# A fused two-block kernel: scanning one projection group ahead, conditioning products spread out, index scores on stacked operands

## What is computed

```python
mod = silu(c) @ w_ada + b_ada                       # 6 x 1024 values
h = rmsnorm(x) * (1 + scale_m) + shift_m
z, xbc, dt_raw, u_pool, gates = split(h @ w_in)     # 2048, 3072, 32, 1024, 2048 columns
xbc = silu(causal_conv(xbc));  dt = softplus(dt_raw + dt_bias)
y = ssd_chunked_scan(x * dt, dt * a, b, c)          # 4 groups of 8 heads x 4 chunks of 128
y = rmsnorm(y * silu(z), per group) @ w_branch_ssd
x = x + gate_m * (sig(g0) * y + sig(g1) * pool(u_pool)) @ w_out   # then the feed-forward part
```

```python
s = einsum('qhd,sd->qhs', q_idx, k_idx) * 64**-0.5   # 8 index heads of 64, one key
score = einsum('qh,qhs->qs', w_idx * 8**-0.5, relu(s));  _, idx = top_k(score, 128)
```

## Time and profile before

| | |
|---|---|
| median of 3 runs | 2499.92 us (2499.48 to 2509.1) |
| profiled execution | 2502.64 us |
| span of its trace | 2500.6 us |
| TensorE, VectorE, ScalarE, GpSimd busy | 96%, 55%, 43%, 16% |
| mean granted TensorE clock | 0.977 |
| chain that ended last: TensorE, VectorE, ScalarE | 82%, 6%, 5% |

### The profile page before, as it was taken

How to read it: one execution, slowest core, us unless ns; L and a number is a source line. 1 busy time by engine, 2 the same in 40 slices (tenths; PEclk the granted TensorE clock), 3 DMA queues, 4 the chain that set the end, 5 groups by cost and what they waited for, 6 DMA issues and landing times.

```text
span 2500.6 us, 41318 instructions
## 1 busy us (share of the span) xinstructions
PE 2396.1 (96%) x15443; PEld 2139.1 (86%) x15443; DVE 1370.8 (55%) x2095; ACT 1062.9 (43%) x1910; POOL 397.1 (16%) x350
## 2 busy tenths in 40 slices
PE   6999999998999999998989999999999989999998
PEld 5778777887899899887868999999988779999987
DVE  5896777223465245457744666643344445766621
ACT  5646764333343233224444333322455554333322
POOL 0000444700410100100121211100100002211100
PEclk8999999999999999998989999999999999999999
DMA  8564433332233352332202233323422112232332
GB/s 291 167 204 103 108 77 85 92 101 83 85 97 93 97 136 86 99 109 57 52 18 64 84 92 86 90 89 91 136 59 62 44 52 85 84 92 85 89 95 92
DMA packets 409481, 238.38 MB, mean 95 GB/s; under 512 B 11434, under 2 KB 400397, under 8 KB 409381
## 3 DMA queue, kind: packets, MB, share of 16 engines
q1 hardware_dynamic: 400549, 202.25, 29.0%
q0 software_dynamic: 8224, 32.61, 3.8%
q10 hardware_dynamic: 608, 2.16, 0.2%
HBM read 234.54 MB, written 5.00 MB: 96 GB/s over the span
## 4 chain that ended last, share of the span: by engine, by line
PE 82%; DVE 6%; ACT 5%; issue 4%; DMA 3%; POOL 0%; SPq 0%; ACTq 0%; DVEq 0%; POOLq 0%
PE PS L508 60%; PE PS L2056 5%; PE PS L1842 3%; DMA w_raw<-in_w_in_dram 2%; ACT w_hi L429 1%; PE PS L2092 1%; PE PS L1857 1%; PE PS L2187 1%; PE PS L1801 1%; PE PS L2134 1%; DVE w_lo L435 1%; PE PS L1921 1%; PE PS L1957 1%; PE PS L2136 1%; PE PS L2071 1%
## 5 line engine op out<-in xcount | busy, mean ns | idle before, releaser
L435 DVE TENSOR_TENSOR w_lo<-w_raw,w_hi 128x1024 fp32r<-128x1024 f32 (+2 forms) x376 | 469.8, 1250 | 631.0 <-ACT w_hi L429 629.7
L508 PE MATMUL PS<-op_hi,w_hi 128*128 128x264 f32 (+3 forms) x2440 | 601.5, 310 | 16.2 <-DVE w_lo L435 13.4
L508 PE MATMUL PS<-op_lo,w_hi 128*128 128x264 f32 (+3 forms) x2440 | 599.0, 309 | 0.0
L508 PE MATMUL PS<-op_hi,w_lo 128*128 128x264 f32 (+3 forms) x2440 | 596.2, 308 | 0.0
L429 ACT ACTIVATE w_hi<-w_raw 128x1024 fp32r<-128x1024 f32 (+2 forms) x376 | 379.4, 1009 | 313.2 <-PE PS L508 261.6
L508 PEld LDWEIGHTS PS<-op_hi,w_hi 128*128 128x128 f32 x2440 | 397.6, 189 | 47.7 <-DVE w_lo L435 16.2
L508 PEld LDWEIGHTS PS<-op_hi,w_lo 128*128 128x128 f32 x2440 | 397.4, 189 | 22.6
L508 PEld LDWEIGHTS PS<-op_lo,w_hi 128*128 128x128 f32 x2440 | 397.0, 189 | 21.8 <-issue 0.5
L508 PE MATMUL PS<-ff_hi,w_lo 128*128 128x512 f32 (+1 forms) x784 | 240.3, 343 | 0.0
L508 PE MATMUL PS<-ff_hi,w_hi 128*128 128x512 f32 (+1 forms) x784 | 239.9, 342 | 0.0
L508 PE MATMUL PS<-ff_lo,w_hi 128*128 128x512 f32 (+1 forms) x784 | 239.9, 342 | 0.0
(11 more groups left out here) (497 smaller groups left out, 3866.2 us busy)
## 6 DMA issues: line engine op xcount, KB each, us to landing
w_raw<-in_w_up_dram SPq DMA_DIRECT2D x120, 512.0 KB, 3.8
w_raw<-in_w_in_dram SPq DMA_DIRECT2D x64, 512.0 KB, 4.1
w_raw<-in_w_down_dram SPq DMA_DIRECT2D x64, 512.0 KB, 3.8
w_ada<-in_w_ada_dram POOLq DMA_DIRECT2D x12, 2048.0 KB, 9.1
decay<-sums_scratch SPq DMA_DIRECT2D x16, 512.0 KB, 5.2
w_raw<-in_w_branch_ssd_dram SPq DMA_DIRECT2D x16, 512.0 KB, 4.0
w_raw<-in_w_in_a_dram SPq DMA_DIRECT2D x16, 512.0 KB, 3.8
w_raw<-in_w_kv_b_dram SPq DMA_DIRECT2D x16, 512.0 KB, 3.9
```

Of the source, the lines that this page charges most:

```text
L435: dve.tensor_tensor(wlo[slot][:, 0:ks, :], wraw[slot][:, 0:ks, :], whi[slot][:, 0:ks, :].bitcast(F32), ALU.subtract).then_inc(sem("w_split ...
L508: last = pe.matmul(a[0:l.cols, h, 0:cn], w[slot][:, k, 0:l.cols], x[:, kk, c0:c0 + cn], start=(j == 0 and k == 0 and w is whi and x is l.h ...
```

## The change

1. dt's split weight gets buffers of its own (`wd_hi`, `wd_lo`). The weight of xbc group 1 is split into slot 0 while the joint group still runs: ScalarE before its fifth h tile, VectorE before the second half of the modulation columns.
2. `modulation(4)` to `modulation(10)` stand after xbc groups 5, 8, ..., 23, `modulation(11)` after z group 0. VectorE spreads the 64 multiply-adds over 22 groups.
3. z group 0 is multiplied, evacuated and split before the loop; step i handles z group i + 1 (u group i - 15 from step 15 on) and step 23 none. `decays(0)` moves behind the first copies of step 0. u group 0 is evacuated at the end of step 15, after the pad.
4. Index queries are stored in fp32r for each head on all 128 rows, the high part on the head's own 64 rows and the low part on the other 64. The key is stored as `ki_hi` twice and `ki_lo` twice. A score is two accumulating fp32r products of 128 rows. The DMA copy of the key is gone.

The program of the sync queue has no edit.

```diff
@@ -227,6 +227,7 @@
...
+        wd_hi, wd_lo = (at(name, [P, 8, HEADS], F32R, A_MISC + i * 1024) for i, name in enumerate(("w_dt_hi", "w_dt_lo")))
@@ -245,9 +246,9 @@
...
-        iq = at("idx_q", [P, 4, T], F32, F + 16896)
+        idx_q = at("idx_q", [P, QH, T], F32R, F + 85568)
+        ki_hi, ki_lo = (at(name, [P, T], F32R, F + 16896 + i * TILE) for i, name in enumerate(("ki_hi", "ki_lo")))
         kwt = at("ki_wi", [P, T], F32, F + 25344)
-        kid = at("ki_twice", [P, T], F32, F + 27456)
@@ -1093,8 +1094,6 @@
...
             pool.memset(sel_allA[:, 24:32], 1.0).then_inc(sem("B_set"), 1)
-            pool.wait_ge(sem("ki_ready"), 1)
-            pool.dma_start(kid[64:128, :], kwt[0:64, :]).then_inc(sem("kid_in"), 16)
@@ -1164,11 +1163,14 @@
...
             for u in range(2):
                 act.wait_ge(sem(f"w_landed{u}"), 16)
-                cn = P if u else L["dt"].cols
-                act.activation(whi[u][:, :, 0:cn], wraw[u][:, :, 0:cn], ACT.Copy).then_inc(sem("w_hi_ready"), 1)
+                hi, cn = (whi[1], P) if u else (wd_hi, HEADS)
+                act.activation(hi[:], wraw[u][:, :, 0:cn], ACT.Copy).then_inc(sem("w_hi_ready"), 1)
...
             for k in range(KD):
+                if k == 4:
+                    act.wait_ge(sem("w_landed0"), 32)
+                    act.activation(whi[0][:], wraw[0][:], ACT.Copy).then_inc(sem("w_hi_ready"), 1)
                 act.wait_ge(sem("mod_ready"), k // 4 + 1)
@@ -1194,7 +1196,8 @@
...
-            evac_loop(act, L["dt"], dt_in)
+            act.wait_ge(sem("units_done"), 1)
+            dt_in(0, 0, 0)
@@ -1236,7 +1239,10 @@
...
-            decays(0)
+            act.wait_ge(sem("ada_acc"), 12)
+            act.wait_ge(sem("units_done"), L["z"].U0 + 1)
+            act.activation(zT[:, 0, :], acc_view(L["z"], 0), ACT.Copy).then_inc(sem("evacuated"), 1)
+            split_hi(act, L["z"], 0, 0, 0)
             for i in range(24):
                 if i < 16:
                     act.wait_ge(sem("ssd_a"), i + 1)
...
                     act.activation(xsb[:], bank(7), ACT.Copy).then_inc(sem("ssd_x"), 1)
+                    if i == 0:
+                        decays(0)
                     if i < 15:
                         decays(i + 1)
-                if i < 16:
-                    l, g = L["z"], i
-                    dst = zT[:, i, :]
+                if i < 15:
+                    l, g = L["z"], i + 1
+                    dst = zT[:, g, :]
                 else:
-                    l, g = L["u"], i - 16
-                    dst = up[:, i - 16, PAD:UPW]
-                    if i == 16:
-                        act.wait_ge(sem("pool_pad"), 1)
-                act.wait_ge(sem("units_done"), l.U0 + g + 1)
-                act.activation(dst, acc_view(l, g % 2), ACT.Copy).then_inc(sem("evacuated"), 1)
-                split_hi(act, l, g // 2, g % 2, 0)
+                    l, g = L["u"], i - 15
+                    dst = up[:, g, PAD:UPW] if g < KD else None
+                if i < 23 and i != 15:
+                    act.wait_ge(sem("units_done"), l.U0 + g + 1)
+                    act.activation(dst, acc_view(l, g % 2), ACT.Copy).then_inc(sem("evacuated"), 1)
+                if i < 23:
+                    split_hi(act, l, g // 2, g % 2, 0)
                 if 1 <= i <= 16:
                     g, c = STEPS[i - 1]
                     act.wait_ge(sem("ssd_t"), i)
                     act.activation(xbc[:, 4 * g:4 * g + 4, c * P:(c + 1) * P],
                                    bank(3).rearrange("p (t n) -> p t n", t=4), ACT.Copy).then_inc(sem("ssd_yT"), 1)
+                if i == 15:
+                    act.wait_ge(sem("pool_pad"), 1)
+                    act.activation(up[:, 0, PAD:UPW], acc_view(L["u"], 0), ACT.Copy).then_inc(sem("evacuated"), 1)
@@ -1356,8 +1367,10 @@
...
                 if name[0] == "i":
-                    act.activation(halves(iq[:, g, :]), src, ACT.Copy).then_inc(sem("evacuated"), 1)
+                    act.activation(halves(idx_q[0:64, 2 * g, :]), src[0:64], ACT.Copy)
+                    act.activation(halves(idx_q[64:128, 2 * g + 1, :]), src[64:128], ACT.Copy).then_inc(sem("idx_hi"), 1)
                 elif name == "kw":
+                    act.wait_ge(sem("evacuated"), l.G0 + g + 2)
                     act.activation(halves(kwt[0:72, :]), src, ACT.Copy).then_inc(sem("evacuated"), 1)
@@ -1443,6 +1456,9 @@
...
+            act.wait_ge(sem("ki_ready"), 1)
+            act.activation(ki_hi[0:64, :], kwt[0:64, :], ACT.Copy)
+            act.activation(ki_hi[64:128, :], kwt[0:64, :], ACT.Copy).then_inc(sem("idx_hi"), 1)
             for s in range(SLOTS_A):
@@ -1732,9 +1748,10 @@
...
                 for u, l in enumerate((L["dt"], L["xbc"])):
-                    for w, x in ((whi, HH), (whi, HL), (wlo, HH)):
-                        last = pe.matmul(acc_view(l, 0, l.cols), w[u][:, k, 0:l.cols], x[:, k, META:T],
-                                         start=(k == 0 and w is whi and x is HH), stop=(k == KD - 1 and w is wlo))
+                    hi, lo = (whi[1], wlo[1]) if u else (wd_hi, wd_lo)
+                    for w, x in ((hi, HH), (hi, HL), (lo, HH)):
+                        last = pe.matmul(acc_view(l, 0, l.cols), w[:, k, :], x[:, k, META:T],
+                                         start=(k == 0 and w is hi and x is HH), stop=(k == KD - 1 and w is lo))
                     if k == KD - 1:
                         last.then_inc(sem("units_done"), 1)
@@ -1755,9 +1772,11 @@
...
-            products(pe, L["xbc"], None, 8, dt_steps, start=1)
-            for n in range(4, 12):
-                modulation(n)
+                if g >= 5 and (g - 5) % 3 == 0:
+                    modulation(4 + (g - 5) // 3)
+            products(pe, L["xbc"], None, NX, dt_steps, start=1)
+            products_of(pe, L["z"], 0, 0)
+            modulation(11)
             pe.wait_ge(sem("mod_ready"), 3)
             pe.wait_ge(sem("dt_tok"), 4)
             pe.wait_ge(sem("conv_out"), NX + 2)
@@ -1777,10 +1796,10 @@
...
-                if i < 16:
-                    products_of(pe, L["z"], i // 2, i % 2)
-                else:
-                    products_of(pe, L["u"], (i - 16) // 2, i % 2)
+                if i < 15:
+                    products_of(pe, L["z"], (i + 1) // 2, (i + 1) % 2)
+                elif i < 23:
+                    products_of(pe, L["u"], (i - 15) // 2, (i + 1) % 2)
@@ -1892,14 +1911,11 @@
...
-                    rows = slice(64 * e, 64 * e + 64)
-                    q, k = iq[rows, h // 2, q0:q0 + nq], (kid if e else kwt)[rows, :]
-                    if nk <= 512:
-                        last = pe.matmul(PS[:, 4 + 2 * e, 0:nk], q, k[:, 0:nk], start=True, stop=True)
-                    else:
-                        for a in range(2):
-                            last = pe.matmul(PS[:, 4 + 2 * e + a, 0:nk // 2], q, k[:, a * nk // 2:(a + 1) * nk // 2],
-                                             start=True, stop=True)
+                    cn = nk if nk <= 512 else nk // 2
+                    for a in range(nk // cn):
+                        for k in (ki_hi, ki_lo):
+                            last = pe.matmul(PS[:, 4 + 2 * e + a, 0:cn], idx_q[:, h, q0:q0 + nq],
+                                             k[:, a * cn:(a + 1) * cn], start=(k is ki_hi), stop=(k is ki_lo))
                     last.then_inc(sem("idx_ps"), 1)
@@ -2019,7 +2035,7 @@
...
-                    pe.wait_ge(sem("kid_in"), 16)
+                    pe.wait_ge(sem("idx_k"), 1)
                 if s < 4:
                     index_scores(s + 1)
@@ -2285,14 +2301,15 @@
...
             for u in range(2):
                 dve.wait_ge(sem("w_hi_ready"), u + 1)
-                cn = P if u else L["dt"].cols
-                dve.tensor_tensor(wlo[u][:, :, 0:cn], wraw[u][:, :, 0:cn], whi[u][:, :, 0:cn].bitcast(F32),
-                                  ALU.subtract).then_inc(sem("w_split"), 1)
+                hi, lo, cn = (whi[1], wlo[1], P) if u else (wd_hi, wd_lo, HEADS)
+                dve.tensor_tensor(lo[:], wraw[u][:, :, 0:cn], hi[:].bitcast(F32), ALU.subtract).then_inc(sem("w_split"), 1)
             for k in range(2):
                 x_lo(k)
             times_c(dve, link, 3, 0, BY_DVE, BY_DVE)
             for k in range(2, 4):
                 x_lo(k)
+            dve.wait_ge(sem("w_hi_ready"), 3)
+            dve.tensor_tensor(wlo[0][:], wraw[0][:], whi[0][:].bitcast(F32), ALU.subtract).then_inc(sem("w_split"), 1)
             dve.wait_ge(sem("ada_done"), 4)
@@ -2314,7 +2331,6 @@
...
-            post_loop(dve, L["dt"])
@@ -2347,8 +2363,10 @@
...
                 dt_steps(g)
-                n, third = 4 + g // 3, g % 3
-                times_c(dve, link, n, *((0, 2), (2, 5), (5, 8))[third])
+                for n in range(4, 12):
+                    k0, k1 = (min(max(64 * x // 22 - 8 * (n - 4), 0), KD) for x in (g, g + 1))
+                    if k0 < k1:
+                        times_c(dve, link, n, k0, k1)
```

(18 more changed lines are left out.)

## The result

The changed kernel takes 2506.92 us (median of 12 runs), the kernel before 2503.15 (12 runs beside them): ratio 1.0019, 95% interval 1.0010 to 1.0027. That is 3.8 us more, where 4.4 were forecast.

A forecast was written before the change was run, and what follows sets the result against it. TensorE, busy 2396.1 of 2500.6 us, was taken as the bound. The terms -0.6 - 1.6 + 9.9 + 0.8 - 4.1 = +4.4 us gave 2507.0 profiled, 2504.3 on the median (+0.2%), range 2494 to 2514.

The forecast's parts named there:

- Start of the projections: Input projections' start: own dt buffers remove a wait and slow projection, -4.0; joint group later, +0.9; sum -3.1 us.
- Conditioning products: Among xbc projections: six products add 5.1 us, filled waits return 2.6 (bounds 0 and 4.7); xbc end at -0.6.
- Rival 4: xbc stage: VectorE's multiply-adds become the bound, +4.2 us, 2508.5; chance 0.12.
- Last xbc tile to the first product: Before the scan: decay-load chain takes 18.1 us instead of 21.25, -3.1; slow projection +1.5; result -1.6 us.
- Scan step 13: ScalarE waits for u 0's load, holding TensorE before step 14: +8.3, slow clock +1.6, together +9.9 us.
- Gates: Steps 15 to 23 and gates: TensorE waits about 5.7 us before the third gate tile; sum +0.8 us.
- Index scores: Index stage: stacked scores take about 1.0 us a head instead of 1.65; -4.1 us in all, bounds 0 and -7.
- the late key: Index stage: VectorE falls behind in the index projections and the key tile comes late, +1.2 us.
- Rival 3: Index scores: giving up side-by-side heads eats the index gain, 2508.4; chance 0.14.
- Rival 2: After step 13's gap the clock stays low, 5.56 us more per half-clock projection, 2515; chance 0.10.
- shows at the other end, where step 23 has none: Scan's end: the projection done early shortens nothing by itself; TensorE reaches the gates one projection (5.56 us) sooner.
- a difference of 0.5%: Whole kernel: a run must differ by about 0.5% (12.5 us) before a measurement tells it from no change.

The follow-up runs named there:

- experiment 8: Kernel before with only dt's own split-weight buffers and the early split: 2498.97 us, ratio 0.9985.
- run 10: Kernel before with only the conditioning products spread over the input groups, scan and dt buffers as before: 2505.16 us, ratio 1.0011.
- experiment 12: run 6 with the spread undone: products 4 to 10 in a row behind the last xbc tile, 11 behind z 0: 2495.76 us, ratio 0.9976.
- experiment 4: Changed kernel with one load moved: sync queue issues u 0's load ahead of decay load 15: 2496.67 us, ratio 0.9972.
- experiment 1: Kernel before with only the changed kernel's stacked index scores: 2500.23 us, ratio 0.9987.
- experiment 2: Changed kernel with the old index scores, all the rest of the change kept: 2511.64 us, ratio 1.0038.
- run 3: Changed kernel with the scan's order undone (no group projected ahead), the rest kept: 2495.31 us, ratio 0.9969.
- run 6: experiment 4 plus the last norm's reciprocal ahead of step 22's weight split and the first two gate tiles written early: 2488.34 us, ratio 0.9941.
- run 7: run 3 plus run 6's two edits at the gates (reciprocal first, first two gate tiles early): 2495.19 us, ratio 0.9970.
- run 9: run 6 with five of VectorE's eight residual scalings moved behind the index key: 2487.87 us, ratio 0.9945.

## Why the prediction was right, step by step

The time and its sign were right: +4.4 forecast, +3.8 measured (interval 2.5 to 6.8). The step that decides it, the load of u 0 that holds TensorE in step 13, was right in cause and in size. Some of the closeness is luck, as three of the smaller terms show. Against the working:

- **Start of the projections, -3.1 (bounds -4.0 and -1.6).** The dt step behind the next projection stands at 60.73 in the trace after and at 63.69 in the one before: -3.0. Right, with both of its halves: the wait gone, and the joint group 0.7 to 0.8 us later where 0.9 were forecast (experiment 8).
- **Conditioning products, +5.1 - 2.6, xbc end at -0.6.** The end came at 193.03 instead of 194.94, -1.9. The mis-sized term is the waits that the products fill. The products are 4.9 us (0.81 each for 0.85); 2.6 of them were taken to be covered, and a net of 1.1 (-1.9 against the -3.0 of the start) means that 3.8 were in this trace. Over all traces it is nearly all 4.9: from the dt step to the end of the xbc tiles nine with the spread took 131.0 to 132.3 us, and five without it 131.3 to 131.8. The upper bound was 4.7, and I took about half of it. VectorE's idle of 1.62 us once in three groups was the sign that TensorE's products were free there. Rival 4 is out by experiments 10 and 12.
- **Last xbc tile to the first product, 18.1 us.** Measured 18.28 (193.03 to 211.31), with a gap of 2.94 us where 2.7 were forecast; right. The slow clock behind the gap was put at 1.5 and cost twice that: the 16 products took 3.67 instead of 2.00 us, the projection behind them was slow as well, and of a lead of 4.88 us (211.31 for 216.19) 1.75 were left at the transposes of step 0's output (222.66 for 224.41), so 3.1. The term of -1.6 came out at +0.2, outside its bounds. Luck covered it: the term before it was 1.3 us better than forecast, so the two together gave -1.75 where the sum had -2.2.
- **Scan step 13, +9.9.** Step 14 began 7.12 us late, from 1.70 early: +8.8, forecast 8.3; one step further it is 9.14 late: +10.8 in all, forecast 9.9 with a clock term of 1.6, measured 2.0. Shown by experiment 4: one load moved takes 10.1 us off the median.
- **Gates, +0.8.** The wait is 5.78 us, forecast 5.7. The third gate tile is 9.2 us late and the first index projection 10.6 (1081.38 for 1070.80), where the sums gave +7.0 and +8.5. Of the 2.1 missing, 0.5 were there before step 13 (1.7 us early and not 2.2), 0.9 came in it, and 0.8 between it and the gates, where TensorE waits 1.12 us for a low part of u's weight at 413.84, a wait that I had not listed; the clock behind the wait cost 1.4, forecast 1.5.
- **Index scores, -4.1.** From the first index projection to the squares of the heads, the lag shrinks from 10.6 to 6.4 us (1181.24 for 1174.83): -4.2, and experiment 1's trace has -4.0 at the same mark; its median gave -2.7, that of the changed kernel against experiment 2's -4.9. The sum is right and its parts are not. The block of 528 gave -3.0 (forecast -2.9), but only because the trace before had it at half clock; that of 400 -0.8 (forecast -1.5), the shorter two +0.1 (forecast -0.9), and the late key +1.5 (forecast +1.2). The projection behind the last scores, for which the prediction had no term, gave -1.2 (6.04 for 7.28 us), and the stretches between the blocks -0.7.
- **Rival 3.** The medians of experiments 1 and 2 put it aside for the stage as a whole. At full clock its claim holds for the last block: there the row tiles took 8.01 us (experiment 2). The Trainium skill (TensorEngine Tiling (Array Packing), When to Use Tiling) has row tiles for 64 rows; it does not speak of operands stacked on 128, so that it speaks against them was the prediction's reading. The tiles do run side by side, and not for the first pair alone: in experiment 2 the second head of a later pair starts 0.50 us behind the first (1169.26 and 1168.76) and overlaps it. As the prediction read the rule, the block is about as fast as with stacked operands, but only while the clock is full; where it was low the row-tiled block took 2.7 to 2.9 us longer than that.
- **Rival 2** (the clock stays low): out. Behind the 9.84 us gap one projection took 7.11 us, and the next 5.8.

One sentence of the prediction told less than it should. It said that the extra projection done early "shows at the other end, where step 23 has none", and priced that as one wait of 5.7 us. It is more than a wait: there the gain of scanning ahead was paid back. Runs 3, 4, 6 and 7 show it: the gain is 0 with the gates' chain as it is and 6.9 us with the chain shortened. The wait itself fell by 5.1 us (run 4 to run 6); the slow projections behind it and the scatter between executions make up what is beyond that.

So the change is slower because of two places that it did not touch: the sync queue's order, which had a weight load behind a decay load that waits for step 13's mask, and the last norm's chain on VectorE and ScalarE, ahead of the gates. With both mended the same change is 15.2 us (0.6%) faster than the kernel before. The prediction also held that only a difference of 0.5% could be told from none; twelve executions of each kernel told 0.19%.

What stays open: why run 7's two edits, which bring its first index projection 3.6 us sooner, do not show in its time; where run 9's shorter index stage is lost; and what decides whether a block of index scores runs at full or at half clock, since both were seen with the same code. That the spread brings 8.4 us between runs 12 and 6 but costs 2.8 on the kernel before follows the square of experiment 12. The cause, that the projection of z 0 covers the stretch in which run 10 idles, fits the waits there (5.02 and 3.23 us in run 10, 0.49 and 2.72 in run 6); no run put other work in that place.
